# Expert weights into the ring: each 2 MB slot load issued as two transfers of 1 MB

## The reference

```python
def expert_block(args):
    xblk, e = args
    hid = jax.nn.silu(xblk @ w_gate[e]) * (xblk @ w_up[e])
    return hid @ w_down[e]
```

## Time and profile before

| | |
|---|---|
| Device time, median of 3 runs | 2006.6 us (2006.08 to 2011.73) |
| Profiled execution: its own time | 2007.85 us |
| Profiled execution: span of the trace | 2006.0 us |
| PE busy | 1878.6 us, 94% of the span |
| Bytes moved | 603.14 MB, mean 301 GB/s |
| Expert loads into the ring | 188, of 2048 KB |

### The profile page before, as it was taken

How to read it: one execution, slowest core, us unless ns; L and a number is a source line. 1 busy time by engine, 2 the same in 40 slices (tenths; PEclk the granted TensorE clock), 3 DMA queues, 4 the chain that set the end, 5 groups by cost and what they waited for, 6 DMA issues and landing times.

```text
span 2006.0 us, 21237 instructions
## 1 busy us (share of the span) xinstructions
PE 1878.6 (94%) x8098; PEld 957.7 (48%) x8098; DVE 853.2 (43%) x1546; ACT 329.6 (16%) x782; POOL 87.6 (4%) x129
## 2 busy tenths in 40 slices
PE   8999999999999999999999999989999998888877
PEld 4555665445556654856334343333875333323322
DVE  1466988834778887854111111112325111111102
ACT  2452111124521102122101010001002000000000
POOL 4102000001020002100000000000000000000000
PEclk9999999999999999999999999999999999999999
DMA  9314877751168877567999999999356999999996
GB/s 310 94 58 145 301 290 269 258 182 52 58 217 291 293 290 243 163 233 260 358 426 428 428 427 428 427 427 406 136 195 269 406 428 428 428 427 428 428 426 263
DMA packets 149242, 603.14 MB, mean 301 GB/s; under 512 B 16584, under 2 KB 60536, under 8 KB 121232
## 3 DMA queue, kind: packets, MB, share of 16 engines
q1 hardware_dynamic: 144064, 591.43, 75.0%
q0 software_dynamic: 4880, 10.22, 1.9%
q10 hardware_dynamic: 192, 0.05, 0.0%
HBM read 597.67 MB, written 1.10 MB: 298 GB/s over the span
## 4 chain that ended last, share of the span: by engine, by line
PE 63%; DMA 25%; DVE 5%; issue 2%; DVEq 1%; ACT 1%; ACTq 1%; SPq 1%
PE ps L2546 14%; PE ps L935 12%; DMA ring<-in_e_w_up 12%; DMA ring<-in_e_w_gate 12%; PE ps L638 7%; PE ps L1018 5%; PE ps L2359 4%; PE ps L2564 3%; PE ps L2291 3%; PE ps L2374 2%; PE ps L737 2%; PE ps L2480 1%; PE ps L2465 1%; ACTq L1133 1%; DMA ring<-in_e_w_down 1%
## 5 line engine op out<-in xcount | busy, mean ns | idle before, releaser
L2546 PE MATMUL ps<-ring,hT 128*64 128x512 f32 (+1 forms) x1056 | 237.5, 600 | 36.5 <-DMA ring<-in_e_w_gate 18.3
L2564 PE MATMUL ps<-ring,qkT 128*64 128x512 f32 (+1 forms) x1024 | 226.6, 594 | 10.7 <-ACT qkT L2783 7.9
L2546 PE MATMUL ps<-ring,late 128*32 128x512 f32 (+1 forms) x928 | 209.9, 605 | 24.1 <-DMA ring<-in_e_w_up 13.6
L638 PE MATMUL ps<-ring,hT 128*128 128x512 f32 (+1 forms) x384 | 172.5, 593 | 2.2 <-DMA ring<-in_w_in 1.3
L2546 PEld LDWEIGHTS ps<-ring,hT 128*64 128x64 f32 (+1 forms) x1056 | 76.4, 125 | 194.1 <-issue 194.0
L3080 DVE TENSOR_TENSOR qkT<-ps,qkT 128x512 f32<-128x512 f32 (+1 forms) x64 | 44.1, 690 | 256.5 <-PE ps L2564 256.5
L3103 DVE TENSOR_TENSOR qkT<-ps,qkT 128x512 f32<-128x512 f32 (+1 forms) x32 | 22.1, 690 | 292.0 <-PE ps L2546 292.0
L2546 PEld LDWEIGHTS ps<-ring,late 128*32 128x32 f32 (+1 forms) x928 | 66.8, 124 | 161.0 <-issue 160.8
L2564 PEld LDWEIGHTS ps<-ring,qkT 128*64 128x64 f32 (+1 forms) x1024 | 70.8, 123 | 147.1 <-issue 147.1
L1641 DVE SCALAR_TENSOR_TENSOR qkT<-ring,cc,qkT 128x512 f32<-128x512 f32 x168 | 125.8, 749 | 8.6 <-issue 0.4
L3099 DVE TENSOR_TENSOR x<-ps,x 128x1024 f32<-128x1024 f32 x22 | 26.9, 1224 | 196.8 <-PE ps L2465 196.8
(11 more groups left out here) (444 smaller groups left out, 2209.3 us busy)
## 6 DMA issues: line engine op xcount, KB each, us to landing
ring<-in_e_w_down SPq DMA_DIRECT2D x64, 2048.0 KB, 17.1
ring<-in_e_w_up SPq DMA_DIRECT2D x64, 2048.0 KB, 17.5
ring<-in_e_w_gate SPq DMA_DIRECT2D x60, 2048.0 KB, 17.2
ring<-in_ada_w SPq DMA_DIRECT2D x24, 2048.0 KB, 14.0
ring<-in_w_gate SPq DMA_DIRECT2D x16, 1408.0 KB, 8.2
ring<-in_w_up SPq DMA_DIRECT2D x16, 1408.0 KB, 8.3
ring<-in_w_down SPq DMA_DIRECT2D x22, 1024.0 KB, 5.0
ring<-in_w_in SPq DMA_DIRECT2D x8, 2048.0 KB, 11.4
```

The lines of the kernel that those rows point to most:

```text
L638: last = mm(m.ps[:, 4 + i, 0:chunk_width(n)], m.hT[:, j, i * P:(i + 1) * P], w[:, j, :], start=(j == 0), stop=(j == KC - 1))
L2546: last = mm(dst, xg[:, j, at + x * n_tok:at + x * n_tok + place], w(x, j), start=(j == 0), stop=(j == KC - 1))
L2564: lasts[x] = mm(dst, m.hidT[:, j, rows + x * place:rows + (x + 1) * place], half_of(w(x, j), n), start=(j == 0), stop=(j == 3))
```

## The change

Each load of a ring slot becomes two transfers of 1 MB that SP issues one directly after the other, both raising the same `e_full[slot]` by 16. PE therefore waits for 32 for each use of a slot, where it waited for 16. A whole-tensor load is cut in the middle of each partition's row, so that a transfer has 128 rows of 8 KB. A load by halves is cut between the two experts: each transfer has 128 rows of 8 KB as well. What lands where, the order of the loads, and what SP waits for before a load stay as they are. The loads of `ahead` aren't touched.

```diff
     if not halves:
-        return sp.dma_start(m.slot[slot], src.rearrange("(q e) (p j) n -> q e p (j n)", e=2, p=P)[p][f % 2])
-    at = f % 2 * (SLOT // 2)
-    tile = src.rearrange("(q e) (p j) n -> q p e (j n)", e=2, p=P)[p][:, :, at:at + SLOT // 2]
-    return sp.dma_start(m.slot[slot].rearrange("p (e n) -> p e n", e=2), tile)
+        whole, tile = src.rearrange("(q e) (p j) n -> q e p (j n)", e=2, p=P)[p][f % 2], m.slot[slot]
+        for at in (0, SLOT // 2):
+            sp.dma_start(tile[:, at:at + SLOT // 2], whole[:, at:at + SLOT // 2]).then_inc(m.e_full[slot], 16)
+        return
+    whole, tile = src.rearrange("(q e) (p j) n -> q p e (j n)", e=2, p=P)[p], m.slot[slot].rearrange("p (e n) -> p e n", e=2)
+    for e in range(2):
+        at = f % 2 * (SLOT // 2)
+        sp.dma_start(tile[:, e, :], whole[:, e, at:at + SLOT // 2]).then_inc(m.e_full[slot], 16)
...
-                expert_load(sp, m, a, l, 0, f, True, f).then_inc(m.e_full[f], 16)
+                expert_load(sp, m, a, l, 0, f, True, f)
...
-                expert_load(sp, m, a, l, p, f, halves, slot).then_inc(m.e_full[slot], 16)
+                expert_load(sp, m, a, l, p, f, halves, slot)
...
-                    pe.wait_ge(m.e_full[slot], (uses_before(r, p, f) + 1) * 16)
+                    pe.wait_ge(m.e_full[slot], (uses_before(r, p, f) + 1) * 32)
```

## The result

Over 17 runs each, the changed kernel takes 2015.91 us (median; 2013.47 to 2022.61) and the kernel before 2006.19 us (2002.15 to 2014.53). The ratio is 1.0045 with a 95% interval of 1.0036 to 1.0054: 9 us, between 7.2 and 10.8 (the two medians lie 9.7 us apart). The forecast was 2018.0 us, 11.4 us over the median of before and so a little above that interval, with a chance of 0.84 for slower by more than 0.3%. The profiled execution has a span of 2014.5 us, 8.5 more than that of before.

A forecast was written before the change was run, and what follows sets the result against it. The prediction took the stream of weights to bound both expert layers; 139 loads x 0.081 us (0.075 packets, 0.006 flag) = 11.3 us, loads by halves 0.07 us, so 2006.6 + 11.4 = 2018.0 us, range 2012 to 2024.4.

The forecast's parts named there:

- The stream sets the pace of both expert layers: Expert layers, from 1025 and 1595 us: weight loads, not PE, set the 29.37 us pair period, 4.895 us a load.
- An 8 KB packet costs in the long stretches what it costs in the last pairs: Long expert stretches: 8 KB packets run at pair 15's 422 GB/s, 4.970 us a load, 0.075 us more.
- Rival A: Load stream: extra packet cost is that of quiet stretches, 32 to 38 ns a load, 2011.9 us; chance 0.14 with D.
- low estimate of 28 ns a load: Load stream: 3 cycles at 850 MHz for each of 8 more packets, 3.9 us over 139 loads.
- The second flag: Load stream: one more small packet per engine and load, taken as 6 ns.
- the 8 ns of the bound: Load stream: upper bound for the second flag's small packet, equal to one 8 KB packet's excess, 316 - 308 ns.
- 139 loads: Both expert layers: 66 and 73 whole-tensor loads lie in stream-bound stretches, of 164; at 0.081 us each, 11.3 us.
- My mean period of 29.55: Layer 0, 1113.75 to 1350.11 us: average of eight pair periods, used to count the loads in both bound stretches.
- SP's second issue costs nothing: SP's queue: the second MB is issued 0.33 us later, covered by 12 us of other loads where the queue is full.
- PE's wait for DMA up by 11 us: Sign in the changed trace: PE's total wait for DMA rises by 11 us, 0.5 us more in each pair.
- Rival B: Load stream: a fixed cost per transfer, 0.25 us a load, adds 35 us, 2041 us, rate under 415 GB/s; chance 0.04.
- Rival C: Load stream: shorter packets drain better, winning up to 3.8 us, 2002.8 us; chance 0.04.

The follow-up runs named there:

- e3: Kernel before, with pairs 2 to 15 all loaded by halves: 8 KB packets, one 2 MB transfer and one flag per slot; 2014.88 us, ratio 1.0035.
- e4: Changed kernel with each load as four transfers of 512 KB, packets of 4 KB, four flags; 2043.78 us, ratio 1.0189 to the kernel before.
- e1: Changed kernel, but whole-tensor loads cut into even and odd partitions, two 1 MB transfers of 16 KB packets; 2006.87 us, ratio 0.9997 to the kernel before.
- e5: As e4, but whole-tensor loads take every fourth partition per transfer, so packets stay at 16 KB; ratio 1.0003 to the kernel before.
- e12: Changed kernel with eight 256 KB transfers per load, each every fourth partition and half a row, 8 KB packets; 2074.0 us, ratio 1.0338 to the kernel before.
- e9: As e5, with loads by halves also cut by rows into four transfers, so no packet is shorter than in the kernel before; ratio 1.0004 to it.
- e10: As e9 with eight transfers of 256 KB, each every eighth partition; median 2674.1 us, ratio 1.3120 to the kernel before.
- e6: Kernel before, with SP also waiting for the landing of the load two before, from pair 2 on; median 2012.06 us, ratio 1.0027.
- e7: As e6, but SP waits for the landing of the load three before; ratio 1.0007 to the kernel before.
- e8: Changed kernel with e6's wait on the load two before; ratio 1.0064 to the kernel before.

## Why the prediction was right, step by step

- *The stream sets the pace of both expert layers.* Shown. The period of a pair went from 29.37 to 29.83 us (forecast 29.85), and every variant with a clearly lower rate is slower.
- *An 8 KB packet costs in the long stretches what it costs in the last pairs.* Shown: 421 to 422 GB/s against the 422 read from the earlier trace rows; 0.075 us a load against 0.075. The agreement to the last digit is luck: the forecast set a rate (422 GB/s, 4.970 us) against a pair's period (4.895 us), and the two rates by themselves, 422 and 428 GB/s, give 0.070. Rival A, which gave the last pairs no weight, has fallen, and with it the prediction's low estimate of 28 ns a load. That e3 has the same rate with one flag, and e4 the same 9.3 ns for each further packet, makes it the number of packets.
- *The second flag, 0.006 us a load.* Over-sized: e1 and e5 show none, to 0.001 us of stream (85.43 and 85.44 MB). The trace has the increments as packets of 4 bytes with a recorded time of 9 ns each (median), about the 8 ns of the bound, but this time runs beside that of other packets. The term takes 0.8 us off the sum.
- *139 loads.* 139 x 0.075 = 10.4 us lies in the measured interval of 7.2 to 10.8, at its upper end. In the two profiled executions layer 1 gives 6.0 us (73 loads, forecast 5.9) and layer 0 only 2.4 (66 loads, forecast 5.3). The chain of the kernel before shows why, in rows that stood between those of the earlier trace rows:

```profile
1053.47 7.07 PE ps L2546 x31
...
1084.38 7.07 PE ps L2546 x31
...
1289.87 7.07 PE ps L2546 x31
...
1320.78 7.07 PE ps L2546 x31
```

  Two of its periods are 30.91 us, 1.55 more than the others: there the DMA pieces of the chain are 23.26 us long instead of 21.7, and at the same places the distance between the first and the last engine steps up, from 3.32 to 4.87 us at 1074.5 us and from 4.84 to 6.36 at 1315.7. The slowest engine fell back. That execution paid 3.1 us in ten periods (1053.47 to 1350.11), the changed one 1.4 (1052.87 to 1352.54). My mean period of 29.55 contained this; the forecast took it as the same in both. The second reason stands ahead of these periods. The forecast counted every load from 1025 us on, when the engines run full; but full engines don't mean yet that PE waits. In the changed kernel the chain stays with PE until 1052.87, while the kernel before had a DMA piece ahead of its own piece at 1053.47. So the changed kernel is still 0.6 us ahead there, and the loads of that first pair cost it nothing. Whether 8 KB packets make such slips smaller, or one execution merely had more of them, isn't settled. What makes an engine fall back isn't shown either; there is a candidate. The core also fetches its instructions by DMA, in this stretch 16 KB about every 30 us (queue q8 of the page, 70 packets in all), in one packet that takes 1.1 us. The two steps come 4.5 and 2.6 us after the start of such a packet (1070.0 and 1313.1 us), the changed kernel's one step in layer 0, at 1257.8, 2.3 us after one. Most such packets are followed by no step, and the trace doesn't say which engine took them.
- *SP's second issue costs nothing.* Right: the medians to landing are still 16 to 17 us. e12 shows a case in which issues cost: eight of them take 5.33 us, longer than the 4.9 us of a load.
- *PE's wait for DMA up by 11 us.* This row was a poor one to name. The waits of PE's L2550 and L2568 for the loads sum to 65.4 us against 61.9 before. That is 3.5 us where 11 were named. Another 2.9 us stand in the modelled matmul times (PE busy 1881.5 against 1878.6 us), the rest between instructions. The granted clock from 1100 to 1300 us was 0.98 against 1.00, but that costs nothing there: the product pieces of the chain at 1132.39 and 1221.92 take 8.8 us instead of 7.1, and yet the three periods from 1082.70 to 1172.14 are 29.81 us each.
- *Rival B, a fixed cost per transfer,* was to be seen as a rate under 415; e1, e5 and e9 leave nothing of it. *Rival C* needed more than 428 GB/s; no variant had it.

## What to carry to other kernels

When the queue of loads is never empty, count packets and not transfers: a packet here is one contiguous run of a partition's row, and each further one costs about 9 ns on its engine (4 KB, 8 KB and 16 KB runs: 409, 421, 428 GB/s), while up to four transfers and flags in place of one were free; at eight the issuing engine no longer kept ahead. Before cutting a load, look for a place in the trace where the same piece size already flows in a full queue; that row gave this forecast its number. And if a load must be cut by partitions, take every second or every fourth for one transfer, which kept the full rate; neither a half of the range nor every eighth partition did, though every eighth looks evenly spread too.

## What the runs showed of the hardware that was not expected

- Two transfers of 1 MB, for partitions 0 to 63 and 64 to 127, run at 215 GB/s, though both are queued at once: packets of 16 KB take 1227 ns instead of 616. Every eighth partition gives 229 GB/s (e10), every second or fourth 428 (e1, e9).
- An issue on SP takes 0.33 us for a tile over all partitions and 0.47 to 0.54 us for a stepped one (e9, e12).
- The flag increments are packets of 9 ns each, and four times as many of them don't lower the rate (e5).
- Packets have two levels in one layer and with one queue: 426 GB/s in the 4 us from 1000 us on and 421 in the long stretch for 8 KB, 431 and 428 for 16 KB. A limit on the queue wins no time (e6, e7, e8); what the cause is stays open.
- The 16 engines of one load finish up to 6.4 us apart in the kernel before, and from the first to the last load of a long stretch this distance grows (3.31 to 6.38 us and 2.18 to 3.93).
